# Moving the judges of a threshold search from VectorE to GpSimd

## The chip, the cores and the metric

The kernel runs on one core of one Trainium2 chip. The metric is the device time of one execution in microseconds (us), given as the median of three runs. The engines are called as the profile calls them: PE is TensorE's matmul side and PEld its weight load, DVE is VectorE, ACT is ScalarE, POOL is GpSimd, SP is SyncE, whose queue here only starts transfers.

## The reference

One layer of a transformer block over 2048 tokens of width 1024. What matters here is the sparse half of its attention, in which an indexer scores every admissible key and each query keeps its best 256 keys:

```python
def dsa_block(q, k, v, q_idx, k_idx, w_idx, q_pos, slopes, topk):
    rel = jax.nn.relu(jnp.einsum('bqhd,bkd->bqhk', q_idx, k_idx))
    score = jnp.einsum('bqh,bqhk->bqk', w_idx, rel).astype(jnp.float32)
    score = jnp.where(chunk_allowed(q_pos, k_pos)[None], score, -jnp.inf)
    kk = min(topk, L)
    top_val, top_idx = lax.top_k(score, kk)
    ...
```

The reference calls this for each block of 128 queries, with the keys up to the end of that block: block b has 128(b+1) keys. It has 16 index heads. Around it stand a combined input projection, dense differential attention, an output projection and an MLP.

## The kernel before

The kernel runs in stages, each a block of programs for the five engines. The search stage is the function `indexing`, from about 310 to 960 us of the profile. Its engines do three kinds of work at once.

**Scores.** For the blocks b = 2 to 15 (numbered k = 0 to 13) and each of 16 heads, PE multiplies queries and keys into one of two PSUM buffers `isps` (line 1082, up to 1024 keys at a time), ACT applies the relu into one of two buffers `spare` (line 1143), and DVE multiplies by the head's weight and adds into the block's row of scores `rank` (line 1237; the first head, line 1234). There are three row buffers, so the adds of block k wait until block k-3 is done with its row. The queries `iq` come by transfers on SP's queue.

**Searches.** The blocks b = 2 to 11 find their threshold of 256 keys by 24 rounds of bisection; blocks 12 to 15 are searched in a later stage, and their rows are stored to memory by POOL (line 1035). A round is a count and a judge. The count compares the whole row with the threshold and accumulates: 21 of 24 rounds on ACT (line 1150, a Sign with an accumulator, which the profile shows as an ACTIVATE and an ACTIVATION_READ_ACCUMULATOR), three on DVE (line 1252). The judge then moves the threshold up or down by a step: line 1258 compares the count with its bound and line 1259 multiplies by the step and adds to the threshold, each on one column of 128 rows; in three rounds of a block line 1264 also negates the threshold. The next count needs the judge's result. After the last round five passes on DVE (lines 1275 to 1294) make the mask, which POOL stores (line 1030). Blocks alternate between two chains (even and odd k), so at most two searches run at a time; the search of block k waits for the mask of block k-2.

**The rest of the projection.** PE fills in with the matmuls of 17 weight tiles (line 1098, 1632 matmuls of 512 columns), whose results ACT evacuates (lines 1170 and 1174) and DVE splits (line 1301); POOL loads the weights (line 961, split by line 1164 on ACT and line 1297 on DVE) and stores the results in four transfers for each group (line 1023; lines of the value tiles: one, line 1016). At the end POOL loads the stored values back (lines 972 to 998), PE turns them (lines 1114 to 1130), ACT copies them out (line 1159), and POOL makes tables of positions (lines 1004 to 1010).

**Order.** `indexing_streams` makes a `Step` for every piece of work with its engine, an estimated cost, the steps it comes after and a key; `indexing_plan` is a list scheduler over these: at each step it takes, of the streams' next jobs, the one that can begin in the earliest slot (of `INDEX_SLACK` us), and in a slot the one with the lowest key. Keys are shifted for each stream by `INDEX_PLACES`. Every engine then runs its jobs in that order, and waits on semaphores for what a job needs; an engine does not pass over a job that has to wait. The estimated costs only set the order:

```python
last = put(chain, Step("judge", "DVE", 0.505 if lower else 0.314, 0.08, where, [(last, 0.0)], r=r, on_act=on_act, ...
SEEN = dict(PE=0.055, ACT=0.037, DVE=0.035, Q=0.1)
```

The second figure of a step, 0.08 here, is when its result is seen after its end, and `SEEN` is added before a waiting job begins. `Q` is POOL.

Of the kernel before, what the change touches and what calls it, by code (L numbers as in the profile page):

```python
# [31 lines left out]
P = 128  # L32
# [26 lines left out]
PT = 3  # L59
INDEX_SLACK = 0.0347  # L60
REST_FROM, REST_PACE, ROUNDS, INDEX_MASK = 75.86, 12.486, -34.794, 169.04
INDEX_PLACES = dict(index=-17.19, relu=-566.8, add=26.95, chain0=-84.64, chain1=-82.32, keep=-267.36, split=258.6,
                    lo=110.56, mm=-14.26, evac=-14.83, evac_lo=-191.95, store=-481.49, kept_mask=-573.36,
                    weights=-212.32, vload=20.2, ahead=-14.8, vturn=-70.63, vcopy=31.74)
ATT_SLACK = 0.1614
# [583 lines left out]
FULL_TILES = range(R_AV // P, R_AV // P + 4)  # L649
IQU = 3  # L650
EARLY_KEYS, EARLY_UNITS = 6, 2
FIRST_LOADS = 10.0
# [58 lines left out]
def indexing_streams():  # L711
# [10 lines left out]
    for k, b in enumerate(range(2, NB)):  # L722
# [29 lines left out]
        for r in range(TOPK_ROUNDS):  # L752
# [6 lines left out]
            lower = (r + 1) % 8 == 7  # L759
            last = put(chain, Step("judge", "DVE", 0.505 if lower else 0.314, 0.08, where, [(last, 0.0)], r=r, on_act=on_act,  # L760
                                   last=lower, **more))
# [96 lines left out]
def indexing(nc, keep, scr, w_in, ht_hi, ht_lo, rest, before, early):  # L858
# [10 lines left out]
    with ExitStack() as ctx:  # L869
# [3 lines left out]
        def sem(name):  # L873
            return ctx.enter_context(nc.semaphore(name))
# [38 lines left out]
        s_kept = [sem(f"s_rank_kept{n}") for n in range(3)]  # L913
        s_v = sem("s_dve_chain2")
        s_w = sem("s_rest_w_in")
        s_whi = sem("s_rest_w_hi")
# [17 lines left out]
        with nc.Block(no_gpsimd_drain=True) as block:  # L934
# [21 lines left out]
            def _(pool):  # L956
# [6 lines left out]
                stored = [0, 0]  # L963
                kept = [0, 0, 0]

                def load_values(n):
# [45 lines left out]
                for job in plan:  # L1012
# [25 lines left out]
                    elif job.kind == "weights":  # L1038
                        load_w(job.n)
                    elif job.kind == "vload":  # L1040
                        load_values(job.n)
                    elif job.kind == "ahead":
                        load_ahead()
                        places()
# [134 lines left out]
            def _(dve):  # L1179
# [35 lines left out]

                counts, searched = [0, 0], [0, 0]
                for job in plan:
                    if job.kind in ("start", "steps", "count", "judge", "mask"):
                        length, q = P * (job.block + 1), job.k % 2
                        row = ranks[job.k % 3][:, 0:length]  # L1220

                        def col(n, q=q):
                            return tk[:, q, n:n + 1]
# [26 lines left out]
                    elif job.kind == "count" and not job.on_act:  # L1250
                        dve.wait_ge(s_thr[q], job.marks)
                        nc.vector.tensor_scalar(below[:, q, 0:length], row, col(TK_T), None,
                                                ALU.is_ge, ALU.add, accum_out=col(TK_N)).then_inc(s_cnt[q], 1)
                    elif job.kind == "judge":
                        counts[q] += 1
                        dve.wait_ge(s_cnt[q], counts[q])
                        bound = 2 * TOPK - length if job.on_act else TOPK
                        then(nc.vector.tensor_scalar(col(TK_G), col(TK_N), float(bound), 0.5, ALU.is_ge, ALU.subtract))
                        ins = nc.vector.scalar_tensor_tensor(out=col(TK_NT), in0=col(TK_G),  # L1259
                                                             scalar=steps[:, q, job.r:job.r + 1], in1=col(TK_NT),  # L1260
                                                             op0=ALU.mult, op1=ALU.add)
                        if job.last:
                            then(ins)
                            ins = nc.vector.tensor_scalar(col(TK_T), col(TK_NT), -1.0, None, ALU.mult)
                        ins.then_inc(s_thr[q], 1)
                    elif job.kind == "mask":
# [2083 lines left out]
```

## Time and profile before

| | us |
|---|---|
| median of 3 runs (3302.88 to 3307.67) | 3305.68 |
| the profiled execution's own time | 3311.04 |
| its span from first to last instruction | 3309.3 |
| search stage, from about 310 to about 960 | 650 |
| PE / DVE / ACT / POOL busy in 310 to 960 | 636.5 / 580.5 / 553.0 / 155.3 |

The span of the profile is 1.7 us shorter than the execution's own time. An engine's busy time counts its instructions alone; what it waits for is listed apart, put down to the engine or transfer that released it. Matmul ends are modelled and overlap, so a PE that is busy all the time need not run at its peak pace; the weight loads beside it help to tell.

### The profile page before, as it was taken

The page shows a single profiled execution, that of the slowest core. Times are in us where ns is not written, and L with a number is a line of the kernel's source. Part 1 is how long each engine was busy: PE and PEld are TensorE (multiplying, and loading weights), DVE is VectorE, ACT ScalarE, POOL GpSimd, SP SyncE. Part 2 cuts the span into 40 slices and gives each one's busy share as a digit, 9 for nine tenths or more (in the row PEclk, how much of TensorE's full clock was granted, in tenths as well). Part 3 has the DMA queues.
Part 4 walks back from the last instruction along what each step waited for, and adds up shares of the span by engine and source line. Part 5 has one row for each costly group of instructions (what it writes and reads, how often), then busy time and mean ns, then how long its engine had stood idle before and what let it go on. Part 6 is the DMA issues. An engine that isn't in the chain of part 4 may idle for free. (4 is left out here: it accounts for less than half of the span.)

```text
span 3309.3 us, 44362 instructions
## 1 busy us (share of the span) xinstructions
PE 3132.8 (95%) x15808; PEld 2544.1 (77%) x15808; DVE 2439.7 (74%) x4302; ACT 1847.5 (56%) x3103; POOL 442.0 (13%) x713
## 2 busy tenths in 40 slices
PE   5899999999978999999999999999999999999998
PEld 4787888888756777777777787788778878888787
DVE  5544898999956687878776678787877875655676
ACT  4312888899768989898986334322432232222232
POOL 0011233012221000000000000221121210000321
PEclk9999999999979999999999999999999999999999
DMA  7476544233376432211111463544444456655555
GB/s 241 128 247 164 150 135 116 84 102 100 120 204 148 102 74 51 60 43 52 33 38 73 140 221 128 188 150 159 145 163 151 161 196 227 240 188 187 194 203 198
DMA packets 327002, 471.73 MB, mean 143 GB/s; under 512 B 25344, under 2 KB 214992, under 8 KB 326400
## 3 DMA queue, kind: packets, MB, share of 16 engines
q1 hardware_dynamic: 274768, 296.96, 30.0%
q0 software_dynamic: 52016, 171.96, 15.5%
q8 instruction: 125, 2.05, 0.3%
q14 instruction: 93, 0.76, 0.1%
HBM read 311.84 MB, written 156.98 MB: 142 GB/s over the span
## 5 line engine op out<-in xcount | busy, mean ns | idle before, releaser
L2513 PE MATMUL m_ps<-m_h,w_hi 128*128 128x512 f32 x1792 | 557.8, 393 | 20.0 <-DVE w_lo L2115 11.9
L2513 PEld LDWEIGHTS m_ps<-m_h,w_hi 128*128 128x128 f32 x1792 | 338.0, 189 | 95.8 <-DVE w_lo L2115 16.4
L1237 DVE SCALAR_TENSOR_TENSOR rank<-spare,iw,rank 128x1024 f32<-128x1024 f32 (+5 forms) x330 | 331.4, 1021 | 37.9 <-ACT spare L1143 31.3
L2526 PE MATMUL m_ps<-w_hi,a_hi 128*128 128x512 f32 x896 | 350.1, 391 | 6.3 <-DVE w_lo L2344 3.4
L2513 PE MATMUL m_ps<-m_h,w_lo 128*128 128x512 f32 x896 | 350.9, 392 | 0.0
L2526 PE MATMUL m_ps<-w_lo,a_hi 128*128 128x512 f32 x896 | 349.8, 390 | 0.0
L2526 PE MATMUL m_ps<-w_hi,a_lo 128*128 128x512 f32 x896 | 349.6, 390 | 0.0
L1143 ACT ACTIVATE spare<-isps 128x1024 f32<-128x1024 f32 (+5 forms) x352 | 277.6, 820 | 60.7 <-PE isps L1082 37.4
L1082 PE MATMUL isps<-ki,iq 128*128 128x512 f32 (+3 forms) x1216 | 291.4, 373 | 11.9 <-DMA iq<-dram_proj 8.8
L1082 PEld LDWEIGHTS isps<-ki,iq 128*128 128x128 f32 x1216 | 224.6, 190 | 67.4 <-DMA iq<-dram_proj 11.4
L1819 ACT ACTIVATE a_hi<-a_lo 128x2048 fp32r<-128x2048 f32 x56 | 107.3, 1917 | 279.3 <-DMA a_lo<-dram_aop 279.3
L3103 ACT ACTIVATE pt<-tps 128x512 f32<-128x512 f32 (+1 forms) x432 | 232.3, 584 | 55.3 <-PE ops L3055 26.6
L3040 PE MATMUL tps<-ident,probs 128*128 128x128 f32 x1632 | 236.6, 280 | 22.7 <-DVE probs L3271 17.6
L1781 ACT ACTIVATE w_hi<-w_raw 128x512 fp32r<-128x512 f32 x160 | 99.8, 625 | 264.1 <-DVE w_raw L2103 205.2
L3091 ACT ACTIVATE probs<-probs,stat 128x128 f32<-128x128 f32 (+15 forms) x192 | 233.1, 1217 | 20.0 <-DVE stat L3255 17.2
L3040 PEld LDWEIGHTS tps<-ident,probs 128*128 128x128 f32 x1632 | 182.1, 142 | 78.4 <-issue 35.2
L1150 ACT ACTIVATE below<-rank,tk 128x512 int8<-128x512 f32 (+9 forms) x210 | 230.4, 1100 | 19.2 <-DVE tk L1259 18.1
L2341 DVE TENSOR_TENSOR a_lo<-a_lo,a_hi 128x2048 fp32r<-128x2048 f32 x56 | 141.3, 2524 | 113.9 <-ACT a_hi L1819 113.8
L1098 PE MATMUL r_ps<-ht_hi,r_w_hi 128*128 128x512 f32 x544 | 216.4, 398 | 6.0 <-PEq L270 4.9
L1694 POOL DMA_DIRECT2D dram_aop<-a_out x224 | 121.0, 541 | 748.5 <-ACT a_out L1803 275.5
L1098 PE MATMUL r_ps<-ht_hi,r_w_lo 128*128 128x512 f32 x544 | 214.5, 394 | 0.0
L1098 PE MATMUL r_ps<-ht_lo,r_w_hi 128*128 128x512 f32 x544 | 213.8, 393 | 0.0
(317 smaller groups left out, 6594.4 us busy)
## 6 DMA issues: line engine op xcount, KB each, us to landing
w_raw<-in_w_ff SPq DMA_DIRECT2D x136, 512.0 KB, 5.5
dram_aop<-a_out POOLq DMA_DIRECT2D x224, 256.0 KB, 2.6
a_lo<-dram_aop SPq DMA_DIRECT2D x56, 1024.0 KB, 5.6
early_queries<-dram_proj SPq DMA_DIRECT2D x124, 256.0 KB, 4.3
iq<-dram_proj SPq DMA_DIRECT2D x224, 128.0 KB, 2.9
ada_w<-in_w_ada POOLq DMA_DIRECT2D x16, 1024.0 KB, 6.4
dram_proj<-r_ev_hi POOLq DMA_DIRECT2D x104, 128.0 KB, 2.6
dram_proj<-r_ev_lo POOLq DMA_DIRECT2D x104, 128.0 KB, 2.7
```

The source lines that it names most:

```text
L1082: mm = nc.tensor.matmul(sps[:, job.n % 2, a:b], iq[:, job.unit % IQU, job.head % 2, part, :], ki[:, job.c * SCH + a:job.c * SCH + b], star ...
L1098: mm = nc.tensor.matmul(ps[:, job.n % 4, :], a[:, i % 2, job.part, :], b[:, job.g, job.part, :], start=job.part == 0 and m == 0, stop=job. ...
L1143: nc.scalar.activation(spare[:, job.n % 2, 0:job.width], sps[:, job.n % 2, 0:job.width], ACT.Relu).then_inc(s_relu, 1)
L1150: nc.scalar.activation(below[:, q, 0:length].bitcast(I8), ranks[job.k % 3][:, 0:length], ACT.Sign, bias=tk[:, q, TK_NT:TK_NT + 1], accum_o ...
L1237: nc.vector.scalar_tensor_tensor(out=dst, in0=got, scalar=w, in1=dst, op0=ALU.mult, op1=ALU.add).then_inc(s_acc, 1)
L1694: pool.dma_start(scr.aop[op, row:row + P, half * GT:(half + 1) * GT], act_in[:, op, :]).then_inc(q_a[op], 16)
L2341: nc.vector.tensor_tensor(s_lo[:, c % RING], s_lo[:, c % RING].bitcast(F32), s_hi[:, c % RING].bitcast(F32), ALU.subtract).then_inc(c_sl, 1)
L2513: mm = nc.tensor.matmul(ps[:, b], w[:, w1_slot(n, j), k, :], hop[:, j, h, :, k, :], start=fresh and k == 0 and i == 0, stop=k == KH - 1 an ...
L2526: mm = nc.tensor.matmul(ps[:, t], a[:, c % RING, k, t * P:(t + 1) * P], w[:, c % RING, k, :], start=first and i == 0, stop=last and i == 2 ...
L3040: tr = nc.tensor.transpose(tps[:, job.turn % TR, (2 * kk + hh) * P:(2 * kk + hh + 1) * P], probs[:, g.heads[hh] % 4, (job.first + kk) * P: ...
L3091: nc.scalar.activation(row, row, ACT.Exp, bias=stat[:, job.hm % 8, 2:3], scale=-1.0, accum_out=stat[:, job.hm % 8, 3:4]).then_inc(s_exp, 1)
L3103: nc.scalar.activation(pt[:, job.slot % PT, 0:width], tps[:, job.of.turn % TR, 0:width], ACT.Copy).then_inc(s_te, 1)
```

## The change

The judges move from DVE's program to POOL's. POOL has them in the same list with its transfers, at the places that the planner gives them. Where DVE used two operations, POOL uses three (four in the rounds that also negate), and POOL waits on a semaphore of its own, `s_judge`, between them. The planner's cost of a judge changes from 0.314 and 0.505 us on DVE to 0.4 and 0.6 us on POOL. All the planner's shifts, and the width of its slot, have new values, so that the order of all engines in the stage may differ. Counts, masks, transfers and sizes stay.

```diff
-INDEX_SLACK = 0.0347
-REST_FROM, REST_PACE, ROUNDS, INDEX_MASK = 75.86, 12.486, -34.794, 169.04
-INDEX_PLACES = dict(index=-17.19, relu=-566.8, add=26.95, chain0=-84.64, chain1=-82.32, keep=-267.36, split=258.6,
-                    lo=110.56, mm=-14.26, evac=-14.83, evac_lo=-191.95, store=-481.49, kept_mask=-573.36,
-                    weights=-212.32, vload=20.2, ahead=-14.8, vturn=-70.63, vcopy=31.74)
+INDEX_SLACK = 0.0636
+REST_FROM, REST_PACE, ROUNDS, INDEX_MASK = 132.07, 8.185, -26.461, 168.05
+INDEX_PLACES = dict(index=-10.95, relu=-518.06, add=-25.25, chain0=-91.79, chain1=-87.39, keep=-319.67, split=239.2,
+                    lo=191.27, mm=29.75, evac=-79.21, evac_lo=-185.88, store=-387.22, kept_mask=-566.03,
+                    weights=-221.42, vload=-82.91, ahead=56.8, vturn=-270.56, vcopy=-9.75)
...
+JUDGE = 0.4
...
-            last = put(chain, Step("judge", "DVE", 0.505 if lower else 0.314, 0.08, where, [(last, 0.0)], r=r, on_act=on_act,
+            last = put(chain, Step("judge", "Q", JUDGE * (1.5 if lower else 1.0), 0.08, where, [(last, 0.0)], r=r, on_act=on_act,
...
+                def judge(job):
+                    length, q = P * (job.block + 1), job.k % 2
+
+                    def col(n):
+                        return tk[:, q, n:n + 1]
+
+                    def then(ins):
+                        judged[0] += 1
+                        ins.then_inc(s_judge, 1)
+                        pool.wait_ge(s_judge, judged[0])
+
+                    counts[q] += 1
+                    pool.wait_ge(s_cnt[q], counts[q])
+                    bound = 2 * TOPK - length if job.on_act else TOPK
+                    then(nc.gpsimd.tensor_scalar(col(TK_G), col(TK_N), float(bound), 0.5, ALU.is_ge, ALU.subtract))
+                    then(nc.gpsimd.tensor_scalar(col(TK_G), col(TK_G), steps[:, q, job.r:job.r + 1], None, ALU.mult))
+                    ins = nc.gpsimd.tensor_tensor(col(TK_NT), col(TK_NT), col(TK_G), ALU.add)
+                    if job.last:
+                        then(ins)
+                        ins = nc.gpsimd.tensor_scalar(col(TK_T), col(TK_NT), -1.0, None, ALU.mult)
+                    ins.then_inc(s_thr[q], 1)
...
-                    elif job.kind == "judge":
-                        counts[q] += 1
-                        dve.wait_ge(s_cnt[q], counts[q])
-                        bound = 2 * TOPK - length if job.on_act else TOPK
-                        then(nc.vector.tensor_scalar(col(TK_G), col(TK_N), float(bound), 0.5, ALU.is_ge, ALU.subtract))
-                        ins = nc.vector.scalar_tensor_tensor(out=col(TK_NT), in0=col(TK_G),
-                                                             scalar=steps[:, q, job.r:job.r + 1], in1=col(TK_NT),
-                                                             op0=ALU.mult, op1=ALU.add)
-                        if job.last:
-                            then(ins)
-                            ins = nc.vector.tensor_scalar(col(TK_T), col(TK_NT), -1.0, None, ALU.mult)
-                        ins.then_inc(s_thr[q], 1)
```

## Rows read from the trace of the kernel before

**Rows 1.** Busy us by stretch: PE, PEld, DVE, ACT, POOL; clock, DMA share, GB/s.

```profile
350.00:850.00 500.00, 500.00 (x2288) 415.18 (x2287) 455.03 (x980) 448.05 (x719) 114.18 (x204) 1.00 0.39 111
850.00:906.00 56.00, 53.21 (x237) 43.27 (x236) 54.24 (x50) 36.33 (x40) 14.17 (x27) 1.00 0.40 119
906.00:960.00 54.00, 44.67 (x215) 33.64 (x213) 38.91 (x33) 39.17 (x49) 20.52 (x30) 0.94 0.73 213
sum 650.00, PE 636.51 PEld 523.07 DVE 580.47 ACT 552.98 POOL 155.33; mean PE 159.13 PEld 130.77 DVE 145.12 ACT 138.24 POOL 38.83
```

**Rows 2.** Instruction groups on DVE, 310 to 850 us: busy us, mean ns, idle before.

```profile
L1237 DVE SCALAR_TENSOR_TENSOR rank<-spare,iw,rank 128x1024 f32<-128x1024 f32 (+7 forms) x266 | 254.5, 967 | 24.2 <-ACT spare L1143 19.1 <-issue 0.3
L1259 DVE SCALAR_TENSOR_TENSOR tk<-tk,steps 128x1 f32<-128x1 f32 x240 | 52.7, 220 | 8.5
...
L1258 DVE TENSOR_SCALAR tk<-tk 128x1 f32<-128x1 f32 x240 | 35.5, 148 | 14.1 <-ACT below L1150 13.4
...
L1297 DVE TENSOR_TENSOR r_w_lo<-r_w_raw,r_w_hi 128x1024 fp32r<-128x1024 f32 x15 | 18.3, 1219 | 0.0
```

**Rows 3.** Groups by shape, 310 to 960 us: the adds of long rows.

```profile
L1237 DVE SCALAR_TENSOR_TENSOR rank<-spare,iw,rank 128x1024 f32<-128x1024 f32 x150 | 191.1, 1282 | 28.1 <-ACT spare L1143 25.7
...
L1237 DVE SCALAR_TENSOR_TENSOR rank<-spare,iw,rank 128x896 f32<-128x896 f32 x30 | 34.4, 1148 | 1.2 <-ACT spare L1143 0.5
```

**Rows 4.** Line 1030, the stores of the masks: duration min/median/max, first and last start.

```profile
L1030 POOL DMA_DIRECT2D dram_masks<-below x10: 540/574/609, 387.0 to 865.5; - x10
```

**Rows 5.** Waits, 310 to 850 us: who for whom, total us, times, longest.

```profile
ACT spare L1143 <- PE isps L1082: 21.4, 27, 6.4
...
ACT below L1150 <- DVE tk L1259: 18.1, 19, 3.1
...
ACT spare L1143 <- DVE rank L1237: 11.6, 14, 2.1
```

**Rows 6.** Waits, 900 to 960 us.

```profile
PE isps L1082 <- DMA iq<-dram_proj: 8.0, 2, 4.7
```

**Rows 7.** Timeline of POOL, two stretches: start us, us, instruction, idle before.

```profile
1.18 0.29 POOL L288 TENSOR_SCALAR_AFFINE_SELECT ident<-ident 128x128 f32<-128x128 f32 x1 [0.23 <-POOL ident L286]
...
962.73 0.09 POOL L2970 MEMSET bias<- 128x1 f32 x1 [4.49 <-remote]
```

**Rows 8.** Timelines of POOL and DVE in the MLP, and line 2341's durations.

```profile
3110.24 2.49 POOL L1715 TENSOR_TENSOR total<-total,residual 128x1024 f32<-128x1024 f32 x1
...
3110.38 4.49 DVE L2341 TENSOR_TENSOR a_lo<-a_lo,a_hi 128x2048 fp32r<-128x2048 f32 x1
...
L2341 DVE TENSOR_TENSOR a_lo<-a_lo,a_hi x56: 2281/2292/4495, 2680.9 to 3264.3; 128x2048 fp32r<-128x2048 f32 x56
...
3154.30 1.21 DVE L2331 TENSOR_TENSOR w_raw<-w_raw,g 128x1024 f32<-128x1024 f32 x1
...
3154.33 3.44 POOL L1715 TENSOR_TENSOR total<-total,residual 128x1024 f32<-128x1024 f32 x1 [2.38 <-DMA residual<-dram_x]
```

**Rows 9.** Timeline of the search stage, 926 to 933 us, DVE and POOL.

```profile
926.81 4.09 DVE L1237 SCALAR_TENSOR_TENSOR rank<-spare,iw,rank 128x1024 f32<-128x1024 f32 x3
...
929.88 2.77 POOL L1009 CAST early_table<-early_second 128x2048 f32<-128x2048 int32 x1
932.60 0.29 POOL L1010 CAST early_diagonal<-early_diagonal 128x128 f32<-128x128 int32 x1
```

**Rows 10.** Timeline of ACT: first and last pair of successive counts, one chain each.

```profile
329.60 0.18 ACT L1150 ACTIVATION_READ_ACCUMULATOR below<-rank,tk 128x1 f32 x1
...
330.88 0.60 ACT L1150 ACTIVATE below<-rank,tk 128x384 int8<-128x384 f32 x1
...
839.24 0.24 ACT L1150 ACTIVATION_READ_ACCUMULATOR below<-rank,tk 128x1 f32 x1
...
841.19 1.56 ACT L1150 ACTIVATE below<-rank,tk 128x1536 int8<-128x1536 f32 x1
```

**Rows 11.** Line 1023, POOL's stores of results: durations, first and last start.

```profile
L1023 POOL DMA_DIRECT2D dram_proj<-r_ev_hi x104: 527/529/1049, 306.3 to 908.8; - x104
```

More of the change, by code:

```diff
@@ L914, in indexing @@
         s_v = sem("s_dve_chain2")
+        s_judge = sem("s_judge_step")
         s_w = sem("s_rest_w_in")
@@ L964, in _ @@
                 kept = [0, 0, 0]
+                counts, judged = [0, 0], [0]
+                def judge(job):
[16 more added lines that the diff above has]
+                    ins.then_inc(s_thr[q], 1)
                 def load_values(n):
@@ L1039, in _ @@
                         load_w(job.n)
+                    elif job.kind == "judge":
+                        judge(job)
                     elif job.kind == "vload":
@@ L1214, in weights_of_heads @@
                     dve.wait_ge(s_iw, 2)
-                counts, searched = [0, 0], [0, 0]
+                searched = [0, 0]
                 for job in plan:
-                    if job.kind in ("start", "steps", "count", "judge", "mask"):
+                    if job.kind in ("start", "steps", "count", "mask"):
                         length, q = P * (job.block + 1), job.k % 2
```

## The prediction

> **What bounds the stage now.** I read the stage by stretches first [rows 1]. From 350 to 850 us PE is busy all of the 500 us and its weight loads 415.2 us, 0.83 of the time; DVE is busy 0.91 and ACT 0.90. So no engine has much room, but PE has none: work taken off DVE there lets PE do nothing more, it only changes which matmuls are run early. The room is at the ends. The weight loads of the whole stage sum to 523.1 us; at the density of the full stretch, 0.83, they would take 523.1/0.83 = 630 us against 650 us. An order that kept PE full from end to end would save 20 us, and nothing done to DVE can save more.
>
> Why PE is not full at the end is seen on DVE. From 850 to 906 us it is busy 54.2 of 56 us [rows 1], with adds. The last search ends with a mask that POOL stores at 865.5 us [rows 4]; the adds of block 14 go into the row buffer that this search used, and those of block 15 come behind them. That is 16 heads of 1.28 + 1.15 us and 16 of 2 x 1.28 us [rows 3], 80 us: 865.5 + 80 = 945.5, and the stage ends at some 958, with 8.0 us in which PE waited for late queries [rows 6]. So the chain behind the end is: the searches, then 80 us of adds.
>
> What sets the pace of the searches is ACT. Its waits between 310 and 850 us are small: 18.1 us of counts for a judge, 21.4 us of relus for PE, 11.6 us for DVE [rows 5]. Between a count's end and the next count of its chain ACT does other work, 1.28 us at the first pair of counts and 1.71 us at the last [rows 10]: the judge hides in this gap. I took all 223 gaps between the two (merged records left out; their mean is 1.88 us, median about 1.5): 25 are under 0.75 us, 127 under 1.7 us, 160 under 2.05 us.
>
> **What leaves DVE.** 240 judges of 148 + 220 ns are 35.5 + 52.7 = 88.2 us [rows 2], and thirty negations. DVE's 580.5 us [rows 1] become some 490. This gives nothing by itself between 350 and 850 us (PE is full), but scores may be added sooner and matmuls of the projection kept for the end, where PE idles. Of the 20 us I take half, 10 us: the 80 us of adds behind the last search and the late queries stay as they are, and ACT, which sets the searches' pace, loses no work. Bounds: 0 and 20.
>
> **What a judge costs on POOL.** The trace has no such operation. Below: three MEMSETs of one column at 0.09 us [rows 7], 0.27 us. Above: three operations of 128 columns at 0.29 us with a semaphore's 0.23 us before the second and third [rows 7], 1.33 us. One column is nearest to the MEMSET, and the hop stays whatever the size: 3 x 0.1 + 2 x 0.23 = 0.76 us. The planner reckons with 0.4.
>
> **Sharing with DVE.** Behind a running DVE instruction that reads two tensors from SBUF, POOL's operation waits, and the other way round: a_lo on line 2341 takes 2.29 us as a rule, and 4.49 us when it begins 0.14 us after a POOL add of 2.49 us; POOL's add that begins 0.03 us after a DVE product of 1.21 us takes 3.44 us for 2.49 [rows 8]. Each time the later one is longer by about what the earlier one still had to run. The adds of this stage seem to do the same: the POOL copy that starts at 929.88 us lasts 2.77 us, and the third add in front of it ends at 930.90, 1.02 us after the copy's start [rows 9]; that the copy lay idle for this 1.02 us is my reading, since no undisturbed copy of its length stands beside it (128 columns take 0.29 us). The Trainium skill says it as a rule (SBUF — State Buffer, section "Who interferes with whom"): a VectorE instruction with two SBUF inputs and a GpSimd one that reads SBUF exclude one another for the whole instruction of whichever began first. The trace agrees (4.49 us against 2.29). By the rule the sum below is the one with this wait, +17 us; without it, -10 us.
>
> Adds and weight splits, both of two SBUF inputs, fill 254.5 + 18.3 = 272.8 us of the 540 us [rows 2], half of the time, with 0.97 us a piece; a few passes of the masks come on top, so I take 0.54. A POOL operation that comes at a random moment waits 0.54 x 0.97/2 = 0.26 us. If all three did, that is 0.79 us a judge. But the second and third come right behind one that held DVE's next add up: if that add always goes first, they wait 0.52 us each, 0.26 + 2 x 0.52 = 1.3 us. Between the two I take 0.95. Bounds: 0 (the judge falls where DVE has run dry during a count) and three whole adds, 2.9 us. So a judge lasts 0.76 + 0.95 = 1.7 us, from 0.27 to 4.2.
>
> The same wait gives DVE back part of what it saved: 720 operations of some 0.15 us, 0.54 of them in front of an add, are 58 us of the 88. DVE is not the bound either way, so this enters no sum.
>
> **What the longer judge does.** Behind the waiting judge POOL's later transfers queue; for its result waits the count on ACT, and behind that count the relus, then DVE's adds and PE's scores. I lay 1.7 us over the gaps of before. 127 of 223 are shorter, by 80 us in sum (5 us at 0.76, 131 us at 2.05). Two searches ran at once for part of the time (the ten searches' lengths sum to 713 us in 516 us), and a stall for one also lengthens the other's gap: I take three quarters, 60 us. ACT's waits for PE and DVE, 21.4 + 11.6 = 33 us [rows 5], can be used up first. That leaves 27 us of later searches, and with the adds behind them of a later end.
>
> **Sum.** +27 - 10 = +17 us. The profiled execution took 3311.0 us of its own time (span 3309.3), so 3328; the median of the runs is 5.4 us lower, so 3323 us by the median.
>
> **The ordering and the rest.** The new keys cost nothing by themselves. The judges stand in POOL's list: POOL is busy 155 of 650 us [rows 1], and 240 x 1.7 = 408 us more still leave room, but a store of four transfers takes 4 x 0.53 = 2.1 us [rows 11] that a judge can't interrupt; 52 such stores are 109 us of 540, so a judge finds one in front in a fifth of the cases, for 1 us: 0.2 us a judge. The planner puts 2.15 us for a store, so its order allows for it, and I add nothing.
>
> **Rivals.**
> 1. The judge fits its gap: it stays at 0.8 us because judges come when DVE has run dry, or because one column needs the shared access too shortly. Then 5 us of shortfall vanish in ACT's 33 us, and the gain of 10 to 20 us stays: 3286 to 3296 us. For it: DVE idles before the judge already in before, 14.1 us in front of line 1258 [rows 2], waiting for the count. Against: half of the time an add runs. It decides from a judge of about 1.4 us: there 45 us of shortfall, 34 after the overlap, are covered by the 33 us. Chance 0.30, the side of faster.
> 2. Gain and stalls cancel, with a judge around 1.5 us: within 7 us of 3306. Chance 0.15.
> 3. My forecast, the lengthened judge holds ACT up: +7 to +68 us (a judge of 2.15 us gives the last: 148 us of shortfall x 3/4 - 33 - 10), 3313 to 3374 us. Chance 0.47.
> 4. GpSimd's queue holds the stores up: a judge that waits for a late count has a store behind it, the evacuation two groups later waits for that store, and PE's matmuls for the evacuation. At 0.5 us for each of the 68 groups, 34 us: 3330 us with the gain. For it: the stores are all in one list with the judges; against: POOL waits so long for its work that a late store has time. Chance 0.08.
>
> **The numbers.** Half a chance lies above +7 us. Faster, by over 0.2% (6.6 us, about what a measurement of this kernel tells from no change): 0.30; within: 0.15; slower: 0.47 + 0.08 = 0.55. The likeliest is 3323 us. The range is 3290 to 3375 us: its low end is the middle of rival 1 with 16 us gained, the high end a judge of 2.15 us; some 0.08 lies under it and 0.12 above. The likeliest case by itself has 3313 to 3374 us.
>
> **What would show it.** Lines 1258, 1259 and 1264 gone from DVE, and DVE's busy time down by much less than 88 us, with adds of 1024 columns above 1.28 us in the mean where POOL stands in front. POOL's three operations, from the first's start to the third's end, near 1.7 us and spread from 0.8 to 3. ACT's waits of counts for POOL well over 18 us, in sum some 50. The store of the last mask after 865.5 us, and the last add later by as much. If the judge lasts under 1 us, the step on sharing is wrong; if ACT waits long for judges while the stage's end holds, the gaps' cover is larger than 33 us; if PE idles for DVE or late queries instead, the order, not the judge, decided.

## The result and the profile after

The changed kernel took 3434.23 us (median of 4 runs, 3432.21 to 3438.16), the kernel before 3306.68 us beside it: 1.0386 times as long (95% interval 1.0373 to 1.0398), slower by 128 us. The forecast was slower, but 3323 us in a range of 3290 to 3375: the side was right, the size was not. Three executions are left out of every time below (one of dve_one_op at a granted clock of 0.83, one of dve_order_write_only at 0.81, where 0.97 to 0.99 is usual, and one of the kernel before that took 16162 us), so that dve_order_write_only stands on one run.

The profiled execution took 3434.82 us. First the stretches (columns as in [rows 1]); the last two are new, because the stage now ends later:

```profile
350.00:850.00 500.00, 436.30 (x1878) 347.11 (x1877) 312.75 (x416) 369.81 (x620) 325.86 (x797) 0.96 0.32 90
850.00:906.00 56.00, 34.48 (x131) 27.07 (x130) 39.48 (x41) 41.22 (x55) 32.40 (x66) 0.80 0.32 94
906.00:960.00 54.00, 50.49 (x227) 40.62 (x227) 39.10 (x41) 44.92 (x57) 20.40 (x51) 0.99 0.24 64
960.00:1010.00 50.00, 50.00 (x227) 41.17 (x226) 48.35 (x44) 32.05 (x36) 15.18 (x29) 1.00 0.45 133
1010.00:1090.00 80.00, 59.22 (x283) 49.61 (x282) 41.62 (x36) 43.19 (x52) 24.16 (x38) 0.86 0.53 162
```

Between 350 and 850 us PE, full before, is busy 436 of 500 us, and ACT 370 where it was 448 [rows 1]: every engine now waits, and none has become the bound by its own work. PE's granted clock, 1.00 in the first two stretches before, is 0.96 and 0.80 there: PE runs some of its matmuls at the lower of its two levels, 1.2 GHz, as from 876.7 us, behind waits of 2.0 and 4.3 us for ACT. Who waits for whom, 310 to 1090 us (total us, times, longest):

```profile
DVE rank L1264 <- ACT spare L1170: 138.9, 105, 5.4
ACT below L1177 <- POOL tk L985: 121.7, 70, 5.5
PE isps L1109 <- ACT spare L1170: 89.2, 51, 9.6
...
DVE below L1279 <- POOL tk L988: 55.1, 28, 12.4
```

To the end of the searches, 310 to 960 us, ACT's relus wait for PE and DVE:

```profile
ACT spare L1170 <- PE isps L1109: 16.8, 18, 6.4
...
ACT spare L1170 <- DVE rank L1264: 5.7, 10, 1.1
```

In the kernel before, 310 to 960 us:

```profile
DVE rank L1237 <- ACT spare L1143: 31.3, 51, 5.5
...
PE isps L1082 <- ACT spare L1143: 2.2, 4, 1.4
```

ACT's counts wait 121.7 us for judges, where it was 18.1 [rows 5]. Behind each waiting count stand relus, so DVE's adds and PE's scores (line 1109) wait for ACT: 138.9 and 89.2 us, where it was 31.3 and 2.2. The judges' three lines, the masks' stores, the projection's matmuls, the adds and the next stage's first counts, a line's instructions each (duration min/median/max in ns, first and last start):

```profile
L983 POOL TENSOR_SCALAR tk<-tk x240: 213/223/2363, 328.9 to 950.0; 128x1 f32<-128x1 f32 x120
L984 POOL TENSOR_SCALAR tk<-tk,steps x240: 294/299/2503, 329.3 to 951.3; 128x1 f32<-128x1 f32 x120
L985 POOL TENSOR_TENSOR tk<-tk x240: 192/193/1485, 329.9 to 952.3; 128x1 f32<-128x1 f32 x120
...
L1055 POOL DMA_DIRECT2D dram_masks<-below x10: 547/596/1014, 404.3 to 970.4; - x10
...
L1125 PE MATMUL r_ps<-ht_hi,r_w_hi x544: 387/389/767, 295.1 to 1052.4; 128*128 128x512 f32 x182
...
L1264 DVE SCALAR_TENSOR_TENSOR rank<-spare,iw,rank x330: 343/1149/1308, 311.7 to 1051.9; 128x1024 f32<-128x1024 f32 x127, 128x384 f32<-128x384 f32 x8, 128x640 f32<-128x640 f32 x8, 128x896 f32<-128x896 f32 x8
...
L3110 ACT ACTIVATE tie<-rank_in,tk x84: 1667/1864/2102, 1114.0 to 1818.4; 128x1664 int8<-128x1664 f32 x21, 128x1792 int8<-128x1792 f32 x21, 128x1920 int8<-128x1920 f32 x21, 128x2048 int8<-128x2048 f32 x21
```

The same ends in the kernel before:

```profile
L1237 DVE SCALAR_TENSOR_TENSOR rank<-spare,iw,rank x330: 340/1148/1289, 313.6 to 956.1; 128x1024 f32<-128x1024 f32 x127, 128x384 f32<-128x384 f32 x8, 128x640 f32<-128x640 f32 x8, 128x896 f32<-128x896 f32 x8
...
L1098 PE MATMUL r_ps<-ht_hi,r_w_hi x544: 387/389/763, 296.4 to 905.1; 128*128 128x512 f32 x182
...
L3095 ACT ACTIVATE tie<-rank_in,tk x84: 1667/1864/2110, 985.9 to 1693.8; 128x1664 int8<-128x1664 f32 x21, 128x1792 int8<-128x1792 f32 x21, 128x1920 int8<-128x1920 f32 x21, 128x2048 int8<-128x2048 f32 x21
```

This splits the loss by place. The last mask is stored 970.4 - 865.5 = 105 us later [rows 4]; the last add starts 1051.9 - 956.1 = 96 us later, so the tail of adds is 9 us shorter; the next stage starts 1114.0 - 985.9 = 128 us later, so another 32 us are lost behind the last add. There the matmuls of the projection, in PE's order among the delayed scores, run on until 1052.4 instead of 905.1 (the starts of the last), and the loading and turning of the values, which ran beside the adds before, stands behind them.

### The profile page after: what moved, and what is told of

It is laid out like the page before. It is cut to its first block and busy times, and to the rows that moved or that the text cites. A ratio compares the mean times of both kernels' runs of the same rounds, so it can differ in the third digit from the quotient of the medians.

```text
span 3433.0 us, 44602 instructions
## 1 busy us (share of the span) xinstructions
PE 3159.2 (92%) x15808; PEld 2550.4 (74%) x15808; DVE 2370.2 (69%) x3792; ACT 1851.1 (54%) x3103; POOL 723.1 (21%) x1463
## 5 line engine op out<-in xcount | busy, mean ns | idle before, releaser
L1264 DVE SCALAR_TENSOR_TENSOR rank<-spare,iw,rank 128x1024 f32<-128x1024 f32 (+5 forms) x330 | 327.7, 1022 | 145.4 <-ACT spare L1170 138.9
L1109 PE MATMUL isps<-ki,iq 128*128 128x512 f32 (+3 forms) x1216 | 300.6, 385 | 91.1 <-ACT spare L1170 89.2
L1177 ACT ACTIVATE below<-rank,tk 128x384 int8<-128x384 f32 (+9 forms) x210 | 230.2, 1099 | 123.7 <-POOL tk L985 121.7
```

The costliest lines, as they stand in the source:

```text
L1109: mm = nc.tensor.matmul(sps[:, job.n % 2, a:b], iq[:, job.unit % IQU, job.head % 2, part, :], ki[:, job.c * SCH + a:job.c * SCH + b], star ...
L1177: nc.scalar.activation(below[:, q, 0:length].bitcast(I8), ranks[job.k % 3][:, 0:length], ACT.Sign, bias=tk[:, q, TK_NT:TK_NT + 1], accum_o ...
L1264: nc.vector.scalar_tensor_tensor(out=dst, in0=got, scalar=w, in1=dst, op0=ALU.mult, op1=ALU.add).then_inc(s_acc, 1)
```

## The experiments

To compare judges I paired each count with its judge in the order of the program, 240 pairs, and took the time from the end of the count's last record to the start of the judge's first operation (the queue in front) and from there to the end of its last (the judge). The sum is the judge's lateness. All three are means; in relay POOL's passing on counts as part of the judge. "Later" is the ratio's excess times 3307 us; the last two columns are the end of the last count in the trace and the sum of the ten searches' lengths.

| kernel | median us | ratio (95%) | later | queue + judge = lateness, us | last count | searches |
|---|---|---|---|---|---|---|
| before | 3306.7 | | | 0.38 + 0.40 = 0.78 | 845 | 713 |
| dve_one_op | 3309.8 | 1.0003 (0.9991 to 1.0014) | 1 | 0.29 + 0.22 = 0.50 | 845 | 711 |
| relay | 3319.2 | 1.0033 (1.0022 to 1.0045) | 11 | 1.06 | 857 | 730 |
| keys_only | 3322.4 | 1.0042 (1.0022 to 1.0061) | 14 | 0.36 + 0.40 = 0.76 | 840 | 732 |
| one_op | 3348.1 | 1.0121 (1.0092 to 1.0150) | 40 | 0.39 + 0.41 = 0.80 | 855 | 750 |
| write_only | 3353.0 | 1.0134 (1.0071 to 1.0197) | 44 | 0.40 + 0.74 = 1.14 | 860 | 764 |
| write_only_long | 3365.9 | 1.0176 (1.0148 to 1.0204) | 58 | 0.42 + 0.88 = 1.30 | 872 | 779 |
| adds_one_input | 3402.8 | 1.0288 (1.0259 to 1.0316) | 95 | 0.47 + 1.03 = 1.50 | 907 | 817 |
| stores_on_sp | 3421.3 | 1.0342 (1.0312 to 1.0372) | 113 | 0.23 + 1.35 = 1.58 | 930 | 852 |
| two_ops | 3425.2 | 1.0353 (1.0286 to 1.0419) | 117 | 0.53 + 1.17 = 1.70 | 934 | 857 |
| after | 3434.2 | 1.0386 (1.0373 to 1.0398) | 128 | 0.58 + 1.31 = 1.89 | 950 | 883 |
| judges_only | 3449.5 | 1.0428 (1.0397 to 1.0458) | 142 | 0.61 + 1.37 = 1.98 | 961 | 913 |
| planned_04 | 3411.3 | 1.0311 (1.0245 to 1.0376) | 103 | 0.69 + 1.33 = 2.02 | 950 | 915 |
| planned_13 | 3387.1 | 1.0237 (1.0173 to 1.0301) | 78 | 0.63 + 1.39 = 2.02 | 921 | 930 |
| dve_order_write_only | 3340.6 (one run) | | 31 | 0.41 + 0.88 = 1.29 | 884 | 768 |
| dve_order_pool | 3432.2 | 1.0372 (1.0333 to 1.0410) | 123 | 0.59 + 1.36 = 1.95 | 965 | 873 |

**Order or place: keys_only and judges_only.** The kernel before with the new keys, and the changed one with the old keys:

```diff
-INDEX_SLACK = 0.0347   (with REST_FROM to INDEX_PLACES of before)
+INDEX_SLACK = 0.0636   (with REST_FROM to INDEX_PLACES of the change)
```

> The kernel before with the new slot and shifts of the planner alone; the judges stay on DVE. Late-judge theory (in the changed kernel a count waits 1.31 us for three POOL operations and 0.58 us more for the queue in front of them, which lengthens every round): the searches end within 10 us of where they ended before (847 us), and the stage by at most 25 us later, 3306 to 3331 us. Order theory (most of the 127 us lies in the new order itself): 3390 us or more.

> The changed kernel with the planner's slot and shifts of before; the judges run on POOL. Late-judge theory: rounds are as long as in the changed kernel, the last count again ends near 950 us, 3410 to 3450 us. Order theory: 3350 us or less.

The new keys alone cost 14 us, the judges under the old keys 142. In keys_only the searches end at 840, not later than before, and PE is full between 350 and 850 us; but its last projection matmul comes at 933.7, where it was 905.5 (the stretch, then the instructions of the projection, of the adds and of the next stage's first counts):

```profile
350.00:850.00 500.00, 498.73 (x2277) 412.95 (x2277) 453.88 (x983) 445.93 (x718) 111.30 (x200) 1.00 0.39 110
```

```profile
L1098 PE MATMUL r_ps<-ht_hi,r_w_lo x544: 388/392/628, 297.3 to 933.7; 128*128 128x512 f32 x182
...
L1237 DVE SCALAR_TENSOR_TENSOR rank<-spare,iw,rank x330: 344/1147/1287, 313.5 to 945.1; 128x1024 f32<-128x1024 f32 x127, 128x384 f32<-128x384 f32 x8, 128x640 f32<-128x640 f32 x8, 128x896 f32<-128x896 f32 x8
...
L3095 ACT ACTIVATE tie<-rank_in,tk x84: 1667/1864/2105, 999.9 to 1707.1; 128x1664 int8<-128x1664 f32 x21, 128x1792 int8<-128x1792 f32 x21, 128x1920 int8<-128x1920 f32 x21, 128x2048 int8<-128x2048 f32 x21
```

The last mask is stored 3 us sooner than before (862.6 against 865.5 us), the last add starts 11 us sooner (945.1 against 956.1), and the next stage 14 us later (999.9 against 985.9): behind the last add the new keys lose 25 us, by their late values. So 25 of the 32 us that the changed kernel loses there come with the keys. In all the new keys explain about a tenth of the loss; the rest is the judge on POOL. (The planner makes another order of the same keys when it has the judges on another engine, so neither run keeps an order as it was; dve_order_pool below does.)

**How long the judge is: one_op and two_ops.** One operation on POOL (the step added without looking at the count, so no threshold is found), and two operations by another algebra (25 columns of steps instead of 24):

```diff
-then(...is_ge, subtract); then(... steps[r] mult); ins = tensor_tensor(NT, NT, G, add)
+ins = nc.gpsimd.tensor_tensor(col(TK_NT), col(TK_NT), steps[:, q, job.r:job.r + 1], ALU.add)          # one_op
+then(nc.gpsimd.tensor_scalar(col(TK_G), col(TK_N), float(bound), steps[r], ALU.is_ge, ALU.mult))       # two_ops
+ins = nc.gpsimd.tensor_scalar(col(TK_NT), col(TK_NT), col(TK_G), steps[r + 1], ALU.add, ALU.subtract)
```

> The changed kernel, in the same order, with one POOL operation for a judge in place of three (two in the rounds that also negate): the threshold moves by the step without looking at the count, so the search finds nothing; counts, waits and transfers are the same. Late-judge theory: a judge lasts 0.2 us, with its waits for DVE about 0.35 in place of 1.31, some 0.95 us less in each of 120 rounds of a chain: the last count ends 80 to 110 us sooner, 3325 to 3360 us. Queue theory (judges wait behind POOL's transfers): only the 0.58 us in front of a judge matters, and it stays: 3410 us or more.

> The changed kernel, in the same order, with a judge of two POOL operations that gives the same thresholds (compare and multiply by the step in one; add it and take off half a step in the other), one hop fewer. Late-judge theory: the undisturbed judge falls from 0.88 to about 0.6 us and one wait for DVE of three goes, 0.35 to 0.4 us less in the mean, at 98 us for each us 3395 to 3402 us. Rival (the order's tightness decides, not the judge): within 10 us of 3434.

```profile
L983 POOL TENSOR_TENSOR tk<-tk,steps 128x1 f32<-128x1 f32 x240 | 95.9, 409 | 279.6 <-ACT below L1175 257.3 <-DVE below L1277 21.3
```

One operation, 0.41 us in the mean and 0.19 at the median, took away 88 of the 128 us; two took away 11, which the intervals hardly tell from nothing. That is the rival's number, but the judge too had shrunk by less than expected: an undisturbed judge of two still takes 0.79 us, since the second operation with its two column operands is longer, and its mean is 1.17, 0.14 us less than with three.

**The queue: stores_on_sp.** The projection's stores (lines 1041 and 1048) issued from SP's queue in the same order:

```diff
-pool.dma_start(scr.proj[...], ...)
+sp.dma_start(scr.proj[...], ...)   # in the plan's order, between the loads of iq
```

> The changed kernel with the stores of the projection's results (lines 1041 and 1048 of the changed kernel) on SP's queue, at the same places of the plan's order. Queue theory: the waits in front of judges (138 us in sum over 240) fall to under 40 us, and the time by 50 us or more, to 3384 us or less. Late-judge theory: 0.4 us of some 1.9 us goes, worth 20 to 50 us, 3384 to 3414 us; if the new plan's end decides instead, no change.

The queue in front fell from 0.58 to 0.23 us and 3434 to 3421: the queue is worth some 13 us, less than either theory had it, and is not the main cause.

**What the judge waits for: write_only and write_only_long.** Three MEMSETs in place of the three operations, at the same semaphores; no threshold is found. The second version has POOL's undisturbed length, 0.88 us:

```diff
+then(nc.gpsimd.memset(junk[:, 0:144], 0))   # write_only_long: 0:230
+then(nc.gpsimd.memset(junk[:, 0:232], 0))   # write_only_long: 0:312
+ins = nc.gpsimd.memset(col(TK_NT), 0.0)
```

> The changed kernel, in the same order, with each judge's three POOL operations replaced by three MEMSETs with the same waits between them (144 and 232 bytes wide, then one column), which read nothing: the threshold stays at zero and the search finds nothing. From the changed kernel and its one-operation variant the stage grows by some 86 us for 0.88 us of a judge, 98 us for each us. Theory that POOL's reads wait for DVE: the long judges (a tenth above 2.4 us in the changed kernel) vanish, the mean falls to about the median, and the time follows by 98 us for each us, some 3380 to 3395 us if the undisturbed judge still takes 0.9 us. Rival (the long judges come from POOL itself or from its transfers): judges above 2 us stay as they are.

> The write-only judges again (three MEMSETs that read nothing, so that the search finds nothing), now wide enough that a judge lasts the 0.88 us of an undisturbed judge of the changed kernel, in place of 0.74. Theory that waiting for DVE's reads makes most of the loss: 0.14 us at 98 us for each us, 3360 to 3375 us, 60 us or more under the changed kernel. Rival (the judge's own length makes most of it): 3400 us or more.

The groups on POOL between 310 and 960 us, after and then write_only_long (busy us, mean ns, idle before):

```profile
L984 POOL TENSOR_SCALAR tk<-tk,steps 128x1 f32<-128x1 f32 x240 | 113.8, 474 | 23.1
L983 POOL TENSOR_SCALAR tk<-tk 128x1 f32<-128x1 f32 x240 | 89.5, 373 | 177.1 <-ACT below L1177 155.6 <-DVE below L1279 18.5
L985 POOL TENSOR_TENSOR tk<-tk 128x1 f32<-128x1 f32 x240 | 69.5, 290 | 20.0
```

```profile
L985 POOL MEMSET junk<- 128x312 uint8 x240 | 87.6, 365 | 13.8
L984 POOL MEMSET junk<- 128x230 uint8 x240 | 71.4, 298 | 198.2 <-ACT below L1178 180.0 <-DVE below L1280 17.1
...
L986 POOL MEMSET tk<- 128x1 f32 x240 | 24.8, 103 | 13.7
```

After's means lie 0.15, 0.18 and 0.10 us over their medians, 0.223, 0.299 and 0.193: the 0.43 us by which a mean judge (1.31) exceeds an undisturbed one (0.88). The MEMSETs' means lie 5 to 8 ns over their minima (292, 357 and 98 ns), and a tenth of these judges is above 0.89 us, where it is 2.42 after. Of the 720 MEMSETs 237 begin while an add of DVE runs, and none of these takes over 20 ns more than its minimum. Equal undisturbed length, same list, same order: the reads' waits cost 3434 - 3366 = 68 us, over half of the loss. (write_only's 3353 us, under its forecast, goes with a judge of 0.74 us in place of the 0.9 reckoned there.) The timeline of after shows one such wait (start us, duration us):

```profile
601.81 0.21 POOL L983 TENSOR_SCALAR tk<-tk 128x1 f32<-128x1 f32 x1
602.12 1.28 POOL L984 TENSOR_SCALAR tk<-tk,steps 128x1 f32<-128x1 f32 x1
603.49 0.19 POOL L985 TENSOR_TENSOR tk<-tk 128x1 f32<-128x1 f32 x1
...
605.05 0.22 POOL L983 TENSOR_SCALAR tk<-tk 128x1 f32<-128x1 f32 x1 [0.52 <-ACT below L1177]
605.36 0.30 POOL L984 TENSOR_SCALAR tk<-tk,steps 128x1 f32<-128x1 f32 x1
605.75 0.19 POOL L985 TENSOR_TENSOR tk<-tk 128x1 f32<-128x1 f32 x1
...
601.96 1.55 DVE L1264 SCALAR_TENSOR_TENSOR rank<-spare,iw,rank 128x1024 f32<-128x1024 f32 x2 [3.42 <-ACT spare L1170]
605.90 1.28 DVE L1264 SCALAR_TENSOR_TENSOR rank<-spare,iw,rank 128x1024 f32<-128x1024 f32 x1 [2.39 <-ACT spare L1170]
```

The first operation, begun before DVE's adds (601.96), takes its 0.21 us; the second begins within them and takes 1.28 us for 0.30. The judge at 605.05 ends at 605.94 and has no add beside it until 605.90: 0.89 us.

The Trainium skill (SBUF — State Buffer, section "Who interferes with whom") limits the exclusion of a VectorE instruction with two SBUF inputs to GpSimd instructions that read SBUF: the MEMSETs agree (longest 0.79 us, against 2.50 for the reads). The eight MEMSETs that were longer by over 40 ns all began beside DVE's first-head products (line 1262 of that kernel), which read one tensor, as here in write_only_long:

```profile
486.03 0.78 POOL L984 MEMSET junk<- 128x230 uint8 x1 [0.23 <-ACT below L1178]
...
485.84 0.74 DVE L1262 TENSOR_SCALAR rank<-spare,iw 128x1024 f32<-128x1024 f32 x1
```

The same section of the Trainium skill has the other direction too, DVE held up by GpSimd; the adds here don't show it: 1308 ns at most, 1289 before.

**Who holds it: adds_one_input.** DVE's adds as a product with an accumulator, one SBUF input (the row of scores is not summed). Each leaves DVE an extra accumulator read of 83 ns:

```diff
-nc.vector.scalar_tensor_tensor(out=dst, in0=got, scalar=w, in1=dst, op0=ALU.mult, op1=ALU.add)
+nc.vector.tensor_scalar(dst, got, w, None, ALU.mult, ALU.add, accum_out=spare_sum[:, c])
```

> The changed kernel with the real POOL judges, and with the adds of lines 1264 on DVE made into products of one tensor read from SBUF (with an accumulator that nobody reads, so that they run at the same pace); a row then holds its last head alone. Theory that POOL waits for DVE instructions of two SBUF inputs: the adds are the most of these, so the mean judge falls from 1.31 us to about 1.0, and the time to 3360 to 3395 us. Rival (POOL's reads are slow by themselves or wait for any DVE instruction): judge and time as in the changed kernel, 3425 to 3445 us.

```profile
L985 POOL TENSOR_SCALAR tk<-tk,steps 128x1 f32<-128x1 f32 x240 | 78.0, 325 | 23.1
L984 POOL TENSOR_SCALAR tk<-tk 128x1 f32<-128x1 f32 x240 | 71.2, 297 | 197.9 <-ACT below L1178 176.9 <-DVE below L1280 18.4
L986 POOL TENSOR_TENSOR tk<-tk 128x1 f32<-128x1 f32 x240 | 54.6, 228 | 20.0
```

The judge's mean fell from 1.31 to 1.03 us: the adds hold 0.28 of its 0.43 us of waiting, and 3434 - 3403 = 31 us of the time, in spite of 330 x 83 ns = 27 us more work on DVE (3403 is 8 us over the forecast). The rest fits DVE's other instructions of two SBUF inputs (weight splits, passes of the masks), which no run took away; but the traces pair with them. I laid to each read that was over 40 ns longer than the shortest of its line the DVE instruction whose end lies nearest to the point from which that shortest time would have sufficed. In the changed kernel 119 such reads, 73 of 105 us, go with the end of an add; with the adds of one input none does, and 29 of the 36 us that are left go with the masks' passes and the weight splits.

**What the planner reckons: planned_13 and planned_04.** The shifts searched anew by the planner's own end of the stage, once with a judge of 1.3 us, once with the 0.4 us of the change:

```diff
-JUDGE = 0.4
+JUDGE = 1.3      # planned_13; planned_04 keeps 0.4; both with searched shifts
```

> The changed kernel's three POOL operations, planned anew with a judge's cost of 1.3 us, the mean that was measured, and shifts looked for with that cost. The planner puts the stage's end 40 us later than that of the kernel before. Theory that the wrong price made most of the loss: stalls for judges shrink, 3335 to 3365 us. Theory that the latency as such costs, whatever the order: 3400 us or more.

> The changed kernel, still told that a judge costs 0.4 us, with shifts looked for at that price, for which the planner's end is that of the kernel before (the changed kernel's shifts give 40 us more). Theory that the late judges cost the same slip in any order made at this price (the last count came 109 us after its planned time in the changed kernel): 3390 to 3420 us. Theory that the change's shifts were the fault: 3350 us or less.

A search at the change's own cost gave back 25 us, at the true cost 50, between the two theories. How much of the 50 is the cost and how much a better order, stays uncertain, since the intervals of the two overlap. The searches themselves got no shorter (930 in sum against 883); other work was placed better around them: in both the next stage starts 26 us after the start of the last add, where it is 62 in the change. No order tried makes the judges on POOL cheaper than on DVE.

**What DVE gains: dve_one_op.** The kernel before without the comparison (no threshold is found):

```diff
-then(nc.vector.tensor_scalar(col(TK_G), col(TK_N), float(bound), 0.5, ALU.is_ge, ALU.subtract))
-ins = nc.vector.scalar_tensor_tensor(out=col(TK_NT), in0=col(TK_G), ...
+ins = nc.vector.scalar_tensor_tensor(out=col(TK_NT), in0=col(TK_N), ...
```

> The kernel before, in its own order, with a judge on DVE of the second operation alone, which leaves the comparison out, so that the search finds nothing: DVE is relieved of 240 operations of 0.148 us and the judge's 0.40 us falls to 0.22. Theory that PE's fullness leaves nothing to gain from 350 to 850 us: within 6 us of the kernel before. Rival (the searches' latency sets the end before as well, at 98 us for each us of a judge): 15 us or more faster.

```profile
350.00:850.00 500.00, 499.57 (x2284) 414.98 (x2284) 425.37 (x752) 446.29 (x716) 114.01 (x204) 1.00 0.39 111
```

DVE is busy 30 us less, the judge shorter by an operation and a hop, and the time is the same. This relief of DVE, a third of the change's 88 us, is worth nothing here, as PE's full row says.

**The cost of lateness: relay, dve_order_write_only and dve_order_pool.** By now one theory said that each us of lateness costs the same in any order; its rival, that the new order makes it dear. relay is the kernel before, in which POOL passes DVE's judge on by one MEMSET; the other two have the order of before, unchanged, with the planner still told of a judge on DVE, and POOL's judges (write-only of 0.88 us, and real) in that place of POOL's list:

```diff
+pool.wait_ge(s_judge[q], judged[q])                                   # relay
+nc.gpsimd.memset(relay[:, q:q + 1], 0.0).then_inc(s_thr[q], 1)
...
-Step("judge", "Q", JUDGE * (1.5 if lower else 1.0), ...               # dve_order_*
+Step("judge", "DVE", 0.505 if lower else 0.314, ...                   # with the keys of before
```

> The kernel before, in its own order, judges on DVE, with the result of each judge passed on by a POOL MEMSET of one column, which stands in POOL's list where the plan has the judge. DVE keeps its work and POOL reads nothing, so only the latency grows: by some 0.3 us for the two hops and the MEMSET, and by what the judge finds in front of it on POOL. Theory that a judge's latency costs some 99 us for each us above that of the kernel before, in any order: 3335 to 3365 us, and what ACT waits for judges rises from 18 us to 40 or more. Theory that the order of before has 33 us of cover, as the prediction took it: 3315 us or less.

> The same order, with write-only judges of 0.88 us (three MEMSETs, so that the search finds nothing). From a count's end to its judge's end some 1.2 us. Theory of one rate in any order: 0.45 us at 99 us, 3350 us. Theory of a cover in the old order: 0.45 us at 39 us, 3320 to 3330 us. The distance to the run with real judges is what POOL's waiting for DVE costs in this order: 20 us or more if that wait is the largest part of the judge's lateness.

> The judges alone: POOL's three operations stand in POOL's list at the places that the plan of the kernel before gave DVE's judges, and every other engine keeps that plan's order to the last instruction. From a count's end to its judge's end some 1.9 us as in the changed kernel, for 0.78 before. Theory that each us of this costs 99 us in any order: 3410 us or more. Theory that the old order covers part of it (the relay cost 39 us for each us): 3345 to 3385 us, and the order planned for POOL, which puts the next count close behind, is what makes a late judge dear.

Both theories fell: one rate by relay, which added 0.28 us to the mean judge and cost 11 us where 28 were due, and the cover of the old order by dve_order_pool, which with real judges comes to 3432 us, the same as the re-planned 3434. Of dve_order_write_only the stretch and then the waits of counts, 310 to 1000 us:

```profile
350.00:850.00 500.00, 477.11 (x2127) 388.55 (x2127) 358.90 (x464) 417.46 (x681) 274.28 (x878) 0.99 0.37 106
```

```profile
ACT below L1178 <- POOL tk L986: 63.0, 53, 3.9
```

The same of dve_order_pool, its waits 310 to 1090 us:

```profile
350.00:850.00 500.00, 434.18 (x1845) 344.18 (x1845) 310.01 (x415) 364.01 (x611) 328.10 (x790) 0.95 0.32 92
```

```profile
ACT below L1177 <- POOL tk L985: 143.2, 93, 5.4
```

In one order and place, with judges equal but for their reads, ACT's waits more than double and PE loses another 43 us of busy time in this stretch. By the mean, lateness grows dearer. In the order of before: from 0.78 to 1.06 us 11 us, to 1.29 another 20, to 1.95 another 92, that is 39, 87 and 139 us of time per us. In the new order, from keys_only's 0.76: 30 to 1.14, 14 to 1.30, 70 to 1.89, that is 79, 88 and 119 (the first two with wide intervals).

But the mean is the wrong measure, and one_op shows it: its 0.80 us is nearly keys_only's 0.76, and it costs 26 us more. Its lateness has a longer tail: a tenth is above 1.9 us, in keys_only above 1.3. So I laid every lateness of a run over every gap of before (a gap is the time from a count's end to the next count of its chain) and summed what overran:

| | before | one_op | write_only | write_only_long | adds_one_input | two_ops | after | relay | dve_order_write_only | dve_order_pool |
|---|---|---|---|---|---|---|---|---|---|---|
| overrun, us | 12 | 45 | 55 | 67 | 95 | 129 | 157 | 32 | 57 | 158 |
| later, us | 0 | 40 | 44 | 58 | 95 | 117 | 128 | 11 | 31 | 123 |

The times go up with the overrun, one_op among them. This is a reckoning made after the runs; none of them changed the spread at an equal mean on purpose.

## Why the prediction was wrong in size

**DVE's relief.** PE as the bound was right, and DVE's gain of nothing between 350 and 850 us too (dve_one_op). Of the 10 us to be gained at the end the adds show 11 in keys_only, but behind them the values lose 25, so that the new keys cost 14; the text had let them cost nothing by themselves.

**The judge's own cost**, taken as 0.76 us, is 0.88: 0.22 + 0.30 + 0.19 and two hops of 0.09. The operations are longer than the MEMSET that I took, the hops shorter than 0.23.

**Sharing with DVE** exists as the step said, but with 0.43 us in the mean, not 0.95. Just over half of the judges meet nothing (median 0.90) and a tenth are above 2.42; the longest takes 5.7, over the bound of 4.2. The mean judge is 1.31 us where I took 1.7. DVE did not pay for it: the adds of 1024 columns take 1283 ns, 1282 before [rows 3]. So the 58 us that POOL was to take back from DVE are wrong, though they entered no sum.

**The queue** of 0.2 us, left out of the sum, is real: 0.38 us in front before, 0.58 after.

So the errors nearly cancelled: 1.7 us laid over the gaps, 1.31 + 0.58 = 1.89 measured. That the lateness came so near is luck. **The step that failed is "What the longer judge does"**, the one that turns lateness into time: 27 us of later searches, measured 105. Three of its parts, by size:

1. *The cover of 33 us.* ACT's waits for PE and DVE, 21.4 and 11.6 us, were to be used up first. Some 10 us of them were: to the end of the searches, 310 to 960 us, ACT still waits 16.8 and 5.7 us for them. But PE now waits 89 us for ACT, since a count that waits holds back the relus behind it, and two buffers `isps` let PE run no further. A late judge is passed on to PE and comes back as a late relu.
2. *One judge for all gaps.* I laid 1.7 us over the gaps of before: 80 us short. At 1.89 it is 105; with the measured spread, each lateness against each gap in turn, 157. The tail, not the mean, meets the short gaps. The ten searches became 883 - 713 = 170 us longer.
3. *The factor of three quarters* for two searches at once was about right: 170 us in the searches are 105 us at their end, 0.62.

157 x 0.62 = 97 with no cover would have been near the 105 us. Behind it, the 80 us of adds held (970.4 to the last add's end at 1053.2 is 83), but the turn of the values, which I had left under cover, is bare: 32 us. The sum is 105 - 9 + 32 = 128, where the text had 27 - 10 = 17. Most of the last two terms is the keys': in keys_only they are -8 and +25.

By cause the 128 us are 14 for the new keys, 44 for the undisturbed judge on POOL (write_only_long over keys_only, whose orders differ), and 70 for its reads' waits. In the order of before it is 31 for the undisturbed judge (one run) and 92 for the waits, 123 in all. So the waits are over half either way; how the rest is shared between order and judge is less sure. POOL's queue is some 13 us of them (stores_on_sp).

**The rivals.** Rival 4, POOL's queue, was put at 34 us and is 13 (stores_on_sp). Rival 1, a judge that fits, is refuted: even one_op's judge of 0.41 us costs 40, of which the keys have 14. Of my signs, ACT's waits for POOL were right in kind (121.7 where "some 50" stood), and the last mask and the last add are both later, as said. "If PE idles for DVE or late queries instead, the order decided": it idles for ACT, and the order of before loses as much.

**What stays open.** That the price per us of mean lateness grows is measured; that the tail over the gaps is the reason is argued from the spreads. A judge held up by an add also holds the other chain's judge and POOL's stores behind it. The share of the splits and mask passes in the 0.43 us, and why PE's order recovers none of its lost time before the end, were not tried alone. Nor was PE's clock: to the next stage's start its matmuls take 41 us in sum over the medians of their kinds, 19 before, and how much of this reaches the end is not known.

## What to carry to other kernels

A small operation in a chain of round trips is priced by its latency and its tail, not by the busy time that it frees: 30 us taken off a DVE that is not the bound were worth nothing (dve_one_op), and 1.2 us of lateness in 240 judges cost 123 us in an unchanged order (dve_order_pool). Lay the whole spread of the new latency over the gaps, not its mean, and count an engine's waits as cover only if nothing that another engine needs stands behind the waiting instruction in its queue. Before moving short reads to GpSimd, look how much of the time VectorE runs instructions with two SBUF inputs; the operations that only write did not wait for them here.

## What the runs showed of the hardware that was not expected

- The sharing is one-sided for short operations: POOL's one-column reads grew from 0.19 to 0.30 us up to 2.50 us, while DVE's adds of 1024 columns stayed at 1283 ns beside 720 of them. The 66 times that such an add began while one of these reads ran, it took 1298 ns at most.
- POOL's one-column operations cost 0.22 us (two immediates), 0.30 us (one column operand) and 0.19 us (two tensors), with some 0.09 us from the end of one to the start of the next across a semaphore.
- POOL's MEMSETs of 230 and 312 bytes on 128 rows have means of 298 and 365 ns over minima of 292 and 357 ns in the same place: writes alone do not wait for the adds. Eight of 720 were longer by 0.07 to 0.49 us, all beside DVE's first-head products of one tensor.
